# Six-block norms: the 512 tokens' transposes and splits ahead of the others, the shifted value made by two engines, products in the same order

## The reference

```python
def modulate(h, shift, scale):
    return h * (1.0 + scale) + shift

h = modulate(rmsnorm(x, norm_mix_w[i]), sh_m, sc_m)
hc = modulate(rmsnorm(ctx, norm_mix_w[i]), shc_m, scc_m)
# i = 0: ab_mixer(h, hc, ...), i = 1: cd_mixer(h, hc, ...)
x = x + g_f * swiglu(modulate(rmsnorm(x, norm_ffn_w[i]), sh_f, sc_f), w_gate, w_up, w_down)
```

## Time and profile before

| | |
|---|---|
| median of 3 runs | 3703.68 us (3699.19 to 3703.89) |
| the profiled execution | 3697.24 us |
| its span, first to last instruction | 3695.4 us |
| mean granted TensorE clock | 0.959 of full |
| TensorE busy | 3333.0 us, 90% |
| VectorE busy | 1421.2 us, 38% |
| ScalarE busy | 1155.6 us, 31% |

### The profile page before, as it was taken

How to read it: one execution, slowest core, us unless ns; L and a number is a source line. 1 busy time by engine, 2 the same in 40 slices (tenths; PEclk the granted TensorE clock), 3 DMA queues, 4 the chain that set the end, 5 groups by cost and what they waited for, 6 DMA issues and landing times.

```text
span 3695.4 us, 41321 instructions
## 1 busy us (share of the span) xinstructions
PE 3333.0 (90%) x17728; PEld 2698.8 (73%) x17728; DVE 1421.2 (38%) x1934; ACT 1155.6 (31%) x1683; POOL 1.2 (0%) x6
## 2 busy tenths in 40 slices
PE   6886888999998888899998988879999979989998
PEld 5765777777876676777786865668887867668876
DVE  2743433343332533344334137341222444352223
ACT  3414443222234434332223116231112333242222
POOL 0000000000000000000000000000000000000000
PEclk9998989999999999999999989989999989999999
DMA  3211223674231023176621220112222103023332
GB/s 114 68 64 57 80 80 85 174 186 137 86 114 66 12 69 114 35 193 161 179 95 63 69 64 1 58 46 57 69 58 69 63 22 104 34 80 102 93 103 74
DMA packets 408885, 313.82 MB, mean 85 GB/s; under 512 B 23160, under 2 KB 357560, under 8 KB 408448
## 3 DMA queue, kind: packets, MB, share of 16 engines
q1 hardware_dynamic: 407440, 305.72, 28.0%
q10 hardware_dynamic: 1264, 5.47, 0.4%
HBM read 309.01 MB, written 2.15 MB: 84 GB/s over the span
## 4 chain that ended last, share of the span: by engine, by line
PE 49%; DVE 4%; ACT 2%; issue 1%; SPq 0%; DMA 0%; DVEq 0%; ACTq 0%
PE ps L329 15%; PE ps L330 14%; PE ps L331 14%; DVE arena L652 1%; PE ps L2600 1%; PE ps L2240 1%; PE ps L2562 1%; PE ps L1533 1%; DVE hT_lo L664 1%; SPq L2445 0%; PE ps L2519 0%; PE ps L1519 0%; DVE X L981 0%; DVE arena L980 0%; DVE w_lo L288 0%
## 5 line engine op out<-in xcount | busy, mean ns | idle before, releaser
L288 DVE TENSOR_TENSOR w_lo<-raw,w_hi 128x1024 fp32r<-128x1024 f32 (+2 forms) x462 | 534.5, 1199 | 894.5 <-ACT w_hi L276 894.3
L276 ACT CAST w_hi<-raw 128x1024 fp32r<-128x1024 f32 (+2 forms) x462 | 453.3, 1032 | 703.5 <-PE ps L331 511.3
L329 PE MATMUL ps<-hT_hi,w_hi 128*128 128x512 f32 (+1 forms) x1616 | 570.7, 353 | 8.8 <-DVE hT_lo L664 6.5
L330 PE MATMUL ps<-hT_lo,w_hi 128*128 128x512 f32 (+1 forms) x1616 | 566.4, 351 | 0.0
L331 PE MATMUL ps<-hT_hi,w_lo 128*128 128x512 f32 (+1 forms) x1616 | 565.6, 350 | 0.0
L329 PE MATMUL ps<-xT_hi,w_hi 128*128 128x512 f32 x1024 | 423.2, 413 | 35.8 <-DVE arena L694 27.3
L330 PE MATMUL ps<-xT_lo,w_hi 128*128 128x512 f32 x1024 | 403.7, 394 | 0.0
L331 PE MATMUL ps<-xT_hi,w_lo 128*128 128x512 f32 x1024 | 401.9, 392 | 0.0
L329 PE MATMUL ps<-w_hi,hT_hi 128*128 128x512 f32 x904 | 361.0, 399 | 40.3 <-DVE w_lo L288 18.7
L330 PE MATMUL ps<-w_lo,hT_hi 128*128 128x512 f32 x904 | 355.9, 394 | 0.0
L331 PE MATMUL ps<-w_hi,hT_lo 128*128 128x512 f32 x904 | 355.6, 393 | 0.0
(11 more groups left out here) (327 smaller groups left out, 3661.0 us busy)
## 6 DMA issues: line engine op xcount, KB each, us to landing
scratch_sb<-in_ada_w SPq DMA_DIRECT2D x96, 512.0 KB, 4.1
raw<-in_ffn_w_in SPq DMA_DIRECT2D x88, 512.0 KB, 6.4
raw<-in_ffn_w_gate SPq DMA_DIRECT2D x44, 512.0 KB, 4.0
raw<-in_ffn_w_up SPq DMA_DIRECT2D x44, 512.0 KB, 5.2
raw<-in_ffn_w_out SPq DMA_DIRECT2D x20, 1024.0 KB, 5.0
raw<-in_ffn_w_down SPq DMA_DIRECT2D x20, 1024.0 KB, 5.0
raw<-in_ev_w_in SPq DMA_DIRECT2D x16, 1024.0 KB, 5.3
raw<-in_xa_w_kv SPq DMA_DIRECT2D x16, 1024.0 KB, 5.2
```

What stands on the lines that cost most here:

```text
L276: act.copy(self.split_chunk(c)[0][:, half], self.raw_chunk(c)[:, half]).then_inc(self.split_hi, 1)
L288: ins = dve.tensor_tensor(lo[:, half], self.raw_chunk(c)[:, half], hi[:, half].bitcast(F32), ALU.subtract)
L329: pe.matmul(out, w[0], x[0], start=first, stop=False)
L330: pe.matmul(out, w[0], x[1], start=False, stop=False)
```

## The change

In `norm_transpose`:

- ACT scales every second block, DVE the others: 2 and 2 of four (was 1 and 3), 3 and 3 of six (was 2 and 4).
- Groups are ordered: the eight `x` groups first (g 0 to 7), then the eight `side` groups (g 8 to 15). TensorE transposes `x` as soon as the first two blocks of either engine are scaled. With six blocks it turns `x` 0 to 3 into banks 0 to 3, then all side groups (two to a bank, banks 4 to 7), then `x` 4 to 7 into banks 0 to 3 again, each behind the low part of group `g - 4`. With four blocks the eight groups have a bank each.
- With a shift, DVE makes the full values of even `x` groups and ACT those of odd ones and of all side groups (`ACT.Identity` with scale and bias). There are four value buffers instead of two, and the value of `g` waits for the low part of `g - 4`. DVE makes the value of `g + 2` ahead of the low part of `g`.
- Without a shift, `x` groups are as before; side groups now go through a value buffer too (ACT multiplies into it, then copies the high part; DVE subtracts from it).
- Banks 0 to 3 are free for products after the low parts of `x` 4 to 7, banks 4 to 7 after the high parts of the side groups.

`project_feature` and `swiglu` go chunk, token part, half: both products of the 512 tokens, then both of the 256. The cd mixer projects `cdqk` before `cda`, and the loads go with `cdqk`.

```diff
@@ weight_plan @@
-            mix(I["cd_w_in_2"][0], [("cd_a", 2048, 2080, 0), ("cd_qk", 512, 1024, 0), ("cd_g", 1536, 2048, 0),
+            mix(I["cd_w_in_2"][0], [("cd_qk", 512, 1024, 0), ("cd_a", 2048, 2080, 0), ("cd_g", 1536, 2048, 0),
...
@@ norm_transpose @@
+    values = k.arena[:, TALL * D:(TALL + 2) * D].rearrange("p (a b) -> p a b", a=4)
-    groups = [(kk, part) for kk in range(KD) for part in ("x", "side")
-              if any((t < TX) == (part == "x") for t in tiles)]
+    sides = nt > TX
+    nx = 4 if sides else 8
+    groups = [(kk, "x") for kk in range(KD)] + [(kk, "side") for kk in range(KD) if sides]
+    bank = lambda g: k.ps[:, g % nx, :] if g < KD else k.ps[:, 4 + (g - KD) // 2, (g % 2) * SIDE:(g % 2 + 1) * SIDE]
+    value = lambda g: values[:, g % 4, 0:width(g)]
+    by_act = lambda g: g >= KD or bool(shift) and g % 2 == 1
...
-        for t in tiles[1::3]:
+        for t in tiles[1::2]:
             act.mul(xn[:, t, :], k.X[:, t, :], rstd[:, t:t + 1]).then_inc(*s_xn_act.up(1))
...
+        def fill(g):
+            kk, part = groups[g]
             act.wait_ge(*s_tr(g + 1))
+            if g >= 4:
+                act.wait_ge(*s_lo(g - 3))
             if shift:
+                ins = act.activation(value(g), bank(g), ACT.Identity, scale=scale(part, kk), bias=shift(part, kk))
             else:
+                ins = act.mul(value(g), bank(g), scale(part, kk))
+            ins.then_inc(*s_full_act.up(1))
+        def high(g):
+            kk, part = groups[g]
+            dst = k.hi[:, kk, place_of(g)]
+            if shift or g >= KD:
+                act.wait_ge(*full(g))
+                act.copy(dst, value(g)).then_inc(*s_hi.up(1))
+            else:
+                act.wait_ge(*s_tr(g + 1))
+                act.mul(dst, bank(g), scale(part, kk)).then_inc(*s_hi.up(1))
+        for g in range(len(groups)):
+            if g % 2 == 0:
+                for x in (g, g + 1):
+                    if by_act(x):
+                        fill(x)
+            high(g)
...
         if shift:
-            full(0)
+            fill(0)
         for g, (kk, part) in enumerate(groups):
+            if g + 2 < len(groups) and shift and not by_act(g + 2):
+                fill(g + 2)
+            dve.wait_ge(*s_hi(g + 1))
+            if shift or g >= KD:
+                ins = dve.tensor_tensor(lo, value(g), hi.bitcast(F32), ALU.subtract)
...
+        pe.wait_ge(*s_xn(2))
+        pe.wait_ge(*s_xn_act(2))
+        for g in range(nx):
+            turn_group(g)
+        if sides:
+            pe.wait_ge(*s_xn(3))
+            pe.wait_ge(*s_xn_act(3))
+        for g in list(range(KD, len(groups))) + list(range(nx, KD)):
+            turn_group(g)
...
-        k.bank_free[g % 8] = k.h_ready[group] = s_lo(g + 1)
+        k.h_ready[group] = s_lo(g + 1)
+        if g < KD:
+            k.bank_free[g % nx] = s_lo(g + 1)
+        else:
+            k.bank_free[4 + (g - KD) // 2] = s_hi(g + 1)
...
@@ project_feature @@
-    groups = [(i, j, sp) for i in range(n) for j in range(min(2, -(-(cols - i * BCOLS) // P)))
-              for sp in token_spans(*tokens)]
+    groups = [(i, j, sp) for i in range(n) for sp in token_spans(*tokens)
+              for j in range(min(2, -(-(cols - i * BCOLS) // P)))]
...
@@ swiglu @@
-            for half in range(2):
-                for part in range(2 if side else 1):
+            for part in range(2 if side else 1):
+                for half in range(2):
```

More of the change, by code:

```diff
@@ L621, in _ @@
             act.wait_ge(*s_sq(i + 1))
-        a, b = tiles[0], tiles[-1] + 1
         act.activation(rstd[:, a:b], ss[:, a:b], ACT.Ln, scale=1.0 / D,
@@ L642, in _, with fill @@
         dve.wait_ge(*s_rstd(2))
-        for t in (t for i, t in enumerate(tiles) if i % 3 != 1):
+        for t in tiles[0::2]:
             dve.tensor_scalar(xn[:, t, :], k.X[:, t, :], rstd[:, t:t + 1], None, ALU.mult).then_inc(*s_xn.up(1))
-        def full(g):
+        def fill(g):
             kk, part = groups[g]
-            w = SEQ if part == "x" else SIDE
             dve.wait_ge(*s_tr(g + 1))
[L650 to L653, removed]
+            if g >= 4:
+                dve.wait_ge(*s_lo(g - 3))
+            dve.tensor_scalar(value(g), bank(g), scale(part, kk), shift(part, kk), ALU.mult, ALU.add).then_inc(*s_full.up(1))
         if shift:
-            full(0)
+            fill(0)
         for g, (kk, part) in enumerate(groups):
[L658 to L665, removed]
-            else:
-                dve.wait_ge(*s_hi(g + 1))
-                ins = dve.scalar_tensor_tensor(lo, k.ps[:, g % 8, 0:w], scale(part, kk), hi.bitcast(F32),
-                                               ALU.mult, ALU.subtract)
+            hi, lo = k.hi[:, kk, place_of(g)], k.lo[:, kk, place_of(g)]
+            if g + 2 < len(groups) and shift and not by_act(g + 2):
[3 more added lines that the diff above has]
+                ins = dve.tensor_tensor(lo, value(g), hi.bitcast(F32), ALU.subtract)
+            else:
+                ins = dve.scalar_tensor_tensor(lo, bank(g), scale(part, kk), hi.bitcast(F32), ALU.mult, ALU.subtract)
             ins.then_inc(*s_lo.up(1))
@@ L673, in _, with turn_group @@
     def _(pe):
[L674 to L683, removed]
+        def turn_group(g):
+            kk, part = groups[g]
+            if nx <= g < KD:
+                pe.wait_ge(*s_lo(g - nx + 1))
+            for i, t in enumerate(tiles[0:TX] if part == "x" else tiles[TX:]):
+                last = pe.transpose(bank(g)[:, i * P:(i + 1) * P], xn[:, t, kk * P:(kk + 1) * P], k.ident)
+            last.then_inc(*s_tr_side.up(1) if g >= KD else s_tr_x.up(1))
+        pe.wait_ge(*s_xn(2))
[7 more added lines that the diff above has]
+            turn_group(g)
     k.bank_free, k.h_ready = {}, {}
     for g, group in enumerate(groups):
-        k.bank_free[g % 8] = k.h_ready[group] = s_lo(g + 1)
+        k.h_ready[group] = s_lo(g + 1)
[3 more added lines that the diff above has]
+            k.bank_free[4 + (g - KD) // 2] = s_hi(g + 1)
 def take(who, eng, dst, src, scale=1.0):
@@ L2903, in cd_mixer @@
 def cd_mixer(k, W):
-    mod_norm(k, "cd_norm", list(range(TALL)), 1, 0, W["cd_a"])
+    mod_norm(k, "cd_norm", list(range(TALL)), 1, 0, W["cd_qk"])
     A = Arena(k)
@@ L2911, in cd_mixer @@
     tab, yf, chan = A(2 * TX * SEQ), A(KQ, SEQ), start[:, 0:2 * P]
-    project_feature(k, "cda", W["cd_a"], 32, lambda m, a, b: a_low[0:32, a:b], (0, ALL),
+    project_feature(k, "cdqk", W["cd_qk"], 512, lambda m, a, b: qk[:, m, a:b], (0, ALL),
+                    scale=lambda m: 0.125 if m < 2 else 1.0,
                     loads=[(decw[0:32], k.ins["decw"]), (rope, k.ins["axrope"]),
@@ L2915, in cd_mixer @@
                            (later, k.ins["gla_later"])])
-    project_feature(k, "cdqk", W["cd_qk"], 512, lambda m, a, b: qk[:, m, a:b], (0, ALL),
-                    scale=lambda m: 0.125 if m < 2 else 1.0)
+    project_feature(k, "cda", W["cd_a"], 32, lambda m, a, b: a_low[0:32, a:b], (0, ALL))
     lane = Lane(k)
```

15 lines of the change are left out of this document (8 added, 7 removed).

## The result

The changed kernel takes **3674.36 us** (median of 4 runs, 3672.22 to 3676.69); the kernel before 3701.81 (4 runs, 3699.19 to 3703.89, three of them those that the forecast started from). The profiled execution took 3676.69 us.

What follows compares the result with a forecast made beforehand. TensorE, busy 3333.0 of 3695.4 us, was taken as the bound, so time is won only where it idles or runs at half clock. 6.4 + 6.3 + 4.9 + 2.4 - 0.8 - 0.4 = 18.8; 3703.7 - 18.8 = 3684.9, range 3676 to 3692.

Steps and rivals of the forecast that it cites:

- the base: Time of the kernel before from which gains were subtracted: median 3703.7 us, with the profiled execution's 3697.2 as the alternative.
- The walk: Step-by-step timing of shifted six-block norms: in ab and cd, first product starts 12.7 and ends 18.15 us after scaling starts.
- The clock term of glu_norm0: First product of glu_norm0 starts at low clock, losing 1.9 us, so the gain there is 4.9 instead of 6.8.
- The costs of the unshifted norms, -1.2: Norms without shift get slower: 0.4 us each in two of six blocks, 0.1 each in four of four blocks.
- The thin cover of the second chunk in the xa norms: Unshifted six-block norms: second chunk split at 418.7 to 419.7, wanted at 419.3; 0 to -0.4 us each, taken as 0.
- cd order: 0: In the cd mixer, `cdqk` before `cda` leaves the same matmuls ahead of the decay step: 0 us.
- In the old order the first would be wanted at 18.15 and starve: With the old product order, the first side product would be wanted 18.15 us after scaling starts and wait for low parts.
- the bound of 21.5 for the side groups: ACT's eight side groups in shifted six-block norms take at most 7.7 us from 13.75, until 21.5 after scaling starts.
- Low clock in all three, and in glu_norm1: Low clock at first products: three six-block shifted norms, gain 15.0 us, chance 0.18; glu_norm1 too, gain 13.1, chance 0.05.
- Costlier handovers: Rival: waits between engines cost 2 us more in each of three stages, 1 in glu_norm1; gain 12 us, chance 0.12.
- Table loads: Rival: ACT's `Identity` needs another function table than the copy, a load each change; slower, 3726 us, chance 0.03.
- Gains lost at the weights: Rival: later products meet weights not yet split, losing the first product's gain; gain 2 us, 3702, chance 0.06.

Runs made afterwards that it cites:

- half_old: The changed kernel with the loop orders of `project_feature` and `swiglu` turned back to old, `cdqk` still first: 3674.45 us, ratio 0.9938.
- norm_only: The new norm with all product orders as in the kernel before, `cda` ahead of `cdqk`: 3680.81 us, ratio 0.995.
- order_only: The kernel before, its norm kept, with only the new order of products and `cdqk` ahead of `cda`: 3703.20 us, ratio 1.0011.
- before_warm: The kernel before with transposes of groups 8 to 15 issued three times in the three shifted six-block norms: 3702.11 us, ratio 1.001.
- one_engine: The changed kernel with VectorE alone making all eight full values of `x`, in the new order of groups: 3680.98 us, ratio 0.9949.

## Why the prediction was right in kind and too small in size

The forecast, 3684.9, lies 10.5 us over the measured 3674.4. Of these, 4.4 are the base, 4.5 are terms of the sum of gains, and 1.6 no row explains (1.6 and 0.6 by the two later medians of after). The steps one by one:

- **The walk** held almost to the tenth: start 12.5 and 12.7 (12.7 forecast), end 18.07 and 18.27 (18.15), VectorE's new wait 1.66 (1.85), the last low part of `x` 14.2 (14.5), high clock in ab and cd. glu_norm1 gained 2.0 at the first product (2.4).
- **The clock term of glu_norm0 failed in size.** Low clock was right (0.77). But the slow stretch of before was taken whole, 1.9; after it lasted 2.7 us, from 2438.68 to 2441.38, and the product took 6.87 us against 5.56 in ab: 1.3. And the start came at 13.21, not 14.05, mostly since the first 40 transposes took 6.25 us here, 6.90 in ab: the clock rose sooner after their start. It ended at 20.1 instead of 21.4, so 6.2 won instead of 4.9.
- **The costs of the unshifted norms, -1.2, are not there.** The first product of xa_norm0 starts at 10.3 (10.18), later by 0.1 instead of 0.4. In xa_norm1 it starts at 10.87 (10.6 to 10.8) in one execution, and at 9.4 in the two others, in which the clock rose 3 us sooner. The stages are equal within their scatter. The thin cover of the second chunk in the xa norms held: no wait for weights there.
- **Ends of first products give 20.9** (6.5, 6.2, 6.2, 2.0), the stages 23.3. The other 2.4 were in no term: 0.9 in cd, where the waits for weights, for low parts and for take-outs fell from 2.2 to 1.3, and 0.4 to 0.6 in each of the others. In ab hardly any of it is near the norm (its products end 6.6 us sooner); it lies behind them, where the two profiles of before differ by 0.9. In glu0 and glu1 no row explains it.
- **So the sum, 18.8, should have been 23.3**: 1.3 from glu_norm0's clock and start, 1.2 from costs that weren't there, 2.4 behind the first products, less 0.4 of over-estimate in glu_norm1. The mechanism of the sum was right, these sizes were not.
- **The base failed, by as much as the sum.** "Runs of the changed kernel should spread as those did": the three runs had 3703.7 for a median, the 21 of a later series 3699.3. That alone is 4.4 us. The forecast named the profiled execution's 3697.2 as the other end and gave it too little room: with both right it would have been 3699.3 - 23.3 = 3676.0.
- **"cd order: 0"** was wrong as reasoning. It won nothing with the old norm and 4.3 us with the new, 6 as profiled: it buys the time in which the second chunk is split. The argument compared the matmuls ahead of the decay step (the work on `cda` that follows), not the length of the first chunk with the split of the second.
- **"In the old order the first would be wanted at 18.15 and starve"** was refuted by half_old: the bound of 21.5 for the side groups was taken as their time, while the pairs come 1.5 us apart, from 15 on, and a product asks for them one by one.
- **Rivals.** Low clock in all three, and in glu_norm1: not seen, first matmuls 0.47 there. Costlier handovers: not seen. Table loads: none, the value 0.78 us beside the copy's 0.62. Gains lost at the weights: seen only in norm_only, in the one place where a chunk is short.

## What to carry to other kernels

When several engines feed a product slice by slice, first ask which slices the first product needs, and make those ahead of all others; dividing the work on them between engines comes second (here all else in the new norm gave 19 us, the second engine for the values 2 to 4). Whatever starts a product sooner brings its second transfer and split forward as well, so compare the length of the first chunk with the time that the next one takes. Take the base of a forecast from stages that repeat, not from a median of three.

## What the runs showed of the hardware

- **Where the half clock falls moves with the execution, and with changes elsewhere.** xa_norm1's stage was 220.9 to 221.5 us with about 30 us at half clock, or 223.4 to 223.9 with 35.8, in one kernel and the other. The whole kernel before spread from 3694.4 to 3702.4 in 11 runs. Two kernels that leave the recurrence itself alone (order_only, before_warm) both had two more falls in that stage, and both were 3 us longer in it; norm_only and one_engine had one more each, behind a wait of 2.65 us that after has without a fall.
- **Transposes alone raise the clock**, as the earlier trace rows had it. After, in ab_norm, nothing but transposes (TensorE; window, us, busy, granted clock):

```profile
1999.80:2002.00 2.20, 2.19 (x11) 0.50 0.00 0
2002.00:2004.00 2.00, 2.00 (x11) 0.50 0.00 0
2004.00:2006.00 2.00, 2.00 (x18) 0.84 0.00 0
2006.00:2008.00 2.00, 0.93 (x9) 1.00 0.00 0
```

  That disagrees with the Trainium skill (TensorE: Matmul & The Clock Gate, Part 4: PE-mode transpose), which says that full clock does not engage for transposes; for these, 128x128 of float32 by the identity and shown as MATMUL, the rows decide. Whether they use the mode that the page means is not shown.
- **The half clock can begin behind a gap.** After 2.6 us of idle (norm_only) and 3.0 (before_warm) the first two or three matmuls ran at full clock, and only then came 3.4 us at half. After 2.30 us (glu0, after) it had fallen before the first matmul. After 0.95 us it did not fall (ab), nor after 1.49.
- **ScalarE's value**, 512 columns out of PSUM with scale and bias by pointer, takes 0.78 us, against 0.70 with a scale alone. The Trainium skill (ScalarE: Activation LUTs, What ACT_TABLE_LOAD costs) gives some 93 ns for each such operand; the difference of 0.08 is near it. At 256 columns it is 0.05 (0.574 against 0.521, both into a value buffer).
